# Unit outputs by token halves through three PSUM banks, convolution taps in the fourth, earlier U loads

## The chip, the cores and the metric

One core of a Trainium2 chip runs the whole kernel. The metric is the device time of one launch in microseconds (us), the median over several runs.

## The reference, cut to what matters

One inference step of a two-layer decoder trunk on a prompt of 512 tokens and 8 sample tokens. Each layer normalises the residual, projects it by one wide matrix `w_in`, feeds three branches (a state-space branch A, a convolution branch B, cross-attention X) and merges them by gates:

```
h = rmsnorm(x, norm_g)
u_a, z_a, u_b, z_b, q, z_x, g_a, g_b, g_x = split(h @ w_in)
y_a, s_new = s5_branch(u_a, ...)                 # 32 groups, 64 complex states, scan over positions
y_a = gelu(y_a); y_a = y_a * sigmoid(y_a @ w_glu + b_glu)
o_a = (y_a * silu(z_a)) @ w_br_ssm
v_b = u_b[:, :512] * sigmoid(u_b[:, 512:])
c_b = silu(layernorm(causal_depthwise_conv(v_b, width 31)))
o_b = (c_b * silu(z_b)) @ w_br_conv
prob = softmax(q @ mk.T * scale); o_x = (prob @ mv * silu(z_x)) @ w_br_xatt
m = sigmoid(g_a) * o_a + sigmoid(g_b) * o_b + sigmoid(g_x) * o_x
x = x + m @ w_out
```

The layer is done for the prompt and for the samples with the same weights; `mk`, `mv` are projections of a 256-token memory for the prompt and caches for the samples. A last rmsnorm gives the outputs; the new states, convolution buffers and memory keys and values are outputs too.

## The kernel before, in words

**Layout.** Activations are transposed: channels on 128 partitions, tokens along the free axis, in two token halves of 260 (256 of the prompt and 4 samples). `h` and every weight are split into a high and a low part in fp32r, and a product is the sum high by high, low by high, high by low.

**Units.** The product of `h` with 128 columns of `w_in` is a unit: 8 k tiles x 3 parts x 2 token halves = 48 matmuls of 260 columns. `PAIRS` (L283) lists the units of a layer in pairs, named by their kind: v (convolution input and its gate), q, u (state-space input), e (gates of the branches B and X), x, b, a (the `z` paths). After them come the tail (the gates of A and the branch products, in four rounds) and the output product. `split_product` (L716) issues a unit; at each k tile and part it does both token halves with the same weight. Its result goes to `acc_ps[0]` or `acc_ps[1]` in turn, each two PSUM banks, one for each token half; `acc_ready0/1` and `acc_free0/1` are the semaphores. `mp`, the other four banks, serves everything that is not a unit.

**The weight ring.** SyncE loads half a unit of weights into one of four slots of `w_st` (`ring_load`, L350), ScalarE casts it to `w_hi` (`high`, L1145), GpSimd makes `w_lo` (`low`, L605, the subtraction at L610). A load waits until `w_lo` of the slot's earlier content is made, a cast until TensorE has used the slot (`w_half_used` for the first half of a unit, `acc_ready` for the second).

**Orders written by hand.** Each engine works through its own list in order, and what a layer's work stands between is decided there. TensorE's list runs through the units and puts the other work between them: memory keys and values, scores and their transposes, the sample attention (`spread`, `sample_products`, `turn_sample`), the state-space work in two halves of the groups (`turn_inputs`, `state_inputs`, `lag_matrices`, `outputs`). ScalarE (`ready` L1150, `one`, `pair`) casts the ring's next half, waits for a unit, casts another half and evacuates both token halves in one instruction (`to_gate`, `to_q`, `to_u`, `to_z`, `to_v`, `glu_gate`). VectorE's list holds the softmax, the state-space matrices and scans, the convolution and the merge.

**The convolution** (`convolution`, L1641) makes 31 taps per channel tile of 512 prompt tokens: at k = 0 `tensor_scalar`, else `scalar_tensor_tensor` through the helper at L1457. Even taps add into one half of `cacc`, odd ones into the other, both in SBUF, so that two neighbours don't depend on each other (`behind=1`); a last addition puts both sums together into `cv`. The taps are cut into pieces between VectorE's other work (`taps_between`), and some pieces wait at `low_made` until a given `w_lo` is there.

**SyncE's list** holds all other loads too, at the places where the code has them. The state-space input `u` goes through DRAM: `u_scratch` is stored after the u units, and twelve loads with a small row each put it into `U` (L464 to L467), behind the value caches of the samples (`cache_load`); they wait until GpSimd has cleared the borders of `U`. The lag matrices go through `k_scratch` into `Mt` (`toeplitz`, L469 to L481), the state-space output through `y_scratch` back into `u` (L505 to L509), and b1's second unit is loaded behind that.

Of the kernel before, what the change touches and what calls it, by code (L numbers as in the profile page):

```python
# [21 lines left out]
P = 128  # L22
# [3 lines left out]
NB = 8  # L26
# [46 lines left out]
def build(nc, x_prompt, x_sample, mem_prompt, state_ssm_re, state_ssm_im, state_conv, cache_mem_k,  # L73
# [12 lines left out]
    with ctx:  # L86
# [54 lines left out]
        def rr(name, off, shape):  # L141
# [60 lines left out]
        t1 = rr("t1", 10256, [P, QH * (T + 1) * H])  # L202
        t2 = rr("t2", 11408, [P, QH * (T + 1) * H])
# [14 lines left out]
        cacc = at(wd_at, 16 * P, 24 * P, "cacc", [P, 2, T, C])  # L218
# [52 lines left out]
            br_x_done=1 glu_sg=4 br_a_done=4 gate_sg=8 sg_free=16 m_done=8 x_sum=8 z_ev=1 b_ready=24 b_free=24 acc_ready0=32  # L271
            acc_ready1=32 acc_free0=32 acc_free1=32 d_loaded0=80 d_loaded1=80
# [3 lines left out]
        acc_ready, acc_free, d_loaded = ([sm[f"{n}{i}"] for i in range(2)] for n in ("acc_ready", "acc_free", "d_loaded"))  # L276
# [15 lines left out]
        assert unit["out"] + KT == UNITS and use["out"] + KT // 2 == per["acc_ready0"]  # L292
# [24 lines left out]
        def _(sp):  # L317
# [42 lines left out]
            for l in range(LAYERS):  # L360
# [75 lines left out]
                pair("e1")  # L436
                half("e2", 0)
                for b in range(4, NB - 2):
                    wait(sp, l, "kq_done", b - 3)
                    cache_load(cache_mem_k, b)  # L440
                half("e2", 1)
                for b in range(NB - 2, NB):
                    wait(sp, l, "kq_done", b - 3)
                    cache_load(cache_mem_k, b)
# [8 lines left out]
                half("x1", 0)  # L453
# [5 lines left out]
                wait(sp, l, "u_out", 16)  # L459
                wait(sp, l, "U_clear", 1)  # L460
                ug = u_dram.rearrange("(g h) a c -> h g a c", h=H)
                Ug = U[:, :, :, :].rearrange("p q e c -> p (q e) c")
                for t in range(T):
                    sp.dma_start(Ug[t * H:(t + 1) * H, :, NB:NB + C], ug[:, :, t // 4, (t % 4) * C:(t % 4 + 1) * C]).then_inc(sm["U_in"], 16)  # L464
                for a in range(2):
                    sp.dma_start(Ug[0:H, :, 4 * a:4 * a + 4], ug[:, :, a, 4 * C:HC]).then_inc(sm["U_in"], 16)
                    sp.dma_start(Ug[7 * H:P, :, YC + 4 * a:YC + 4 * a + 4], ug[:, :, a, 4 * C:HC]).then_inc(sm["U_in"], 16)  # L467

                def toeplitz(half):  # L469
# [3 lines left out]
                    kg = kh.rearrange("g h x -> h g x")  # L473
                    sp.dma_start(kh.rearrange("(r y) h x -> (y h) r x", r=2), kt[:, :, :]).then_inc(sm["k_out"], 16)
# [12 lines left out]
                pair("e5")  # L487
                pair("e6")
                pair("e7")
                pair("b0")  # L490
                pair("a0")
# [8 lines left out]
                pair("a1")  # L500
# [11 lines left out]
                def glu_loads():  # L512

                    wait(sp, l, "acc_done", 4)
# [81 lines left out]
        def _(pool):  # L596
# [7 lines left out]
            for l in range(LAYERS):  # L604
# [35 lines left out]
                for name in ("u1", "e0", "e1", "e2", "x0"):  # L640
# [3 lines left out]
                wait(pool, l, "pv_done", 1)  # L644
                wait(pool, l, "V_done", 1)
                pool.memset(U[:, :, :, 0:NB], 0.0)
# [1369 lines left out]
```

## Time and profile before

| | |
|---|---|
| median of 3 runs | 1162.32 us (1159.71 to 1163.3) |
| the profiled execution's own time | 1161.13 us |
| its span in the profile | 1159.3 us |
| TensorE matmuls / VectorE / ScalarE / GpSimd busy | 94% / 72% / 36% / 37% of the span |
| granted TensorE clock, mean | 0.975 |

A busy share counts the time in which an instruction of the engine was under way. TensorE's matmuls are pipelined: one takes 0.29 us from its start to its modelled end, while the next starts 0.12 us after it. A wait is put down to the engine and line whose semaphore came last; "DVEq" is VectorE's sequencer (an increment without an instruction), "SPq" the DMA issues of SyncE, "issue" a time in which the profile shows no other releaser. Line numbers can be those of a helper: L1451 is every `tensor_tensor`, L1457 every `scalar_tensor_tensor`, L659 every transpose, L729 every unit product.

### The profile page before, as it was taken

To read this page: it belongs to the slowest core of one execution; us is meant where nothing else is said; L and a number is where in the kernel's file an instruction comes from. 1 tells how busy PE (TensorE), PEld (TensorE's weight loads), DVE (VectorE), ACT (ScalarE), POOL (GpSimd) and SP (SyncE) were. 2 spreads that over 40 slices of the span, in tenths; PEclk is the share of its full clock that TensorE was granted. 3 is DMA by queue.
4 is the path that set the end of the run, shared out by engine and by line. 5 is a ranking of instruction groups with operands and counts; after the bars stand their busy time and mean duration, and the time that the engine had idled before them with its cause. 6 is when DMAs were issued, how large, how long until landed. Compare 5 with 4: busy or idle time off the path is not lost.

```text
span 1159.3 us, 20485 instructions
## 1 busy us (share of the span) xinstructions
PE 1084.3 (94%) x8274; PEld 1015.6 (88%) x8274; DVE 834.0 (72%) x1209; ACT 415.8 (36%) x709; POOL 427.9 (37%) x329
## 2 busy tenths in 40 slices
PE   5999899989989899999989999998998999899995
PEld 3679889979979889999956999897997989899994
DVE  3899989868996684444677998987899668644412
ACT  5423443325443252222433354332535334222222
POOL 0245443524332223444403644353332331344440
PEclk9999999989999999999999999999998999899998
DMA  9345427594317813445532651669531573344422
GB/s 259 100 100 189 145 74 213 191 167 121 99 42 148 231 62 115 130 129 155 152 98 82 173 181 50 196 205 168 133 110 56 124 182 119 103 123 136 135 83 74
DMA packets 225269, 155.01 MB, mean 134 GB/s; under 512 B 48651, under 2 KB 201675, under 8 KB 223111
## 3 DMA queue, kind: packets, MB, share of 16 engines
q1 hardware_dynamic: 219590, 142.04, 44.4%
q10 hardware_dynamic: 5584, 11.67, 2.8%
q8 instruction: 65, 1.06, 0.4%
q14 instruction: 30, 0.24, 0.1%
HBM read 130.38 MB, written 24.24 MB: 133 GB/s over the span
## 4 chain that ended last, share of the span: by engine, by line
PE 51%; DVE 31%; SPq 6%; DMA 6%; issue 4%; ACT 2%; POOL 0%; DVEq 0%; ACTq 0%
PE acc L729 29%; PE mp L1071 12%; DVE cacc L1457 10%; DVE s L1451 4%; DVE X L1451 3%; DMA w_st<-in_w_in 3%; PE mp L768 2%; SPq L464 2%; PE mp L659 2%; DVE tiny L1451 2%; PE acc L1052 1%; SPq L505 1%; PE mp L874 1%; DVE wt L1451 1%; DMA y_scratch<-U 1%
## 5 line engine op out<-in xcount | busy, mean ns | idle before, releaser
L610 POOL TENSOR_TENSOR w_lo<-w_st,w_hi 128x512 fp32r<-128x512 f32 x288 | 403.3, 1406 | 654.4 <-ACT w_hi L1148 654.0
L1148 ACT CAST w_hi<-w_st 128x512 fp32r<-128x512 f32 x288 | 177.6, 622 | 574.1 <-PE acc L729 352.8
L729 PE MATMUL acc<-h_hi,w_hi 128*128 128x260 f32 x1600 | 332.0, 289 | 6.8 <-ACT z L1293 5.9
L729 PE MATMUL acc<-h_hi,w_lo 128*128 128x260 f32 x1600 | 325.2, 285 | 0.0
L729 PE MATMUL acc<-h_lo,w_hi 128*128 128x260 f32 x1600 | 325.1, 285 | 0.0
L729 PEld LDWEIGHTS acc<-h_hi,w_hi 128*128 128x128 f32 x1600 | 250.8, 191 | 15.8 <-issue 7.7
L729 PEld LDWEIGHTS acc<-h_lo,w_hi 128*128 128x128 f32 x1600 | 249.9, 191 | 0.0
L729 PEld LDWEIGHTS acc<-h_hi,w_lo 128*128 128x128 f32 x1600 | 249.9, 191 | 0.0
L1457 DVE SCALAR_TENSOR_TENSOR cacc<-vx,cw,cacc 128x512 f32<-128x512 f32 x232 | 222.7, 1021 | 10.3 <-POOL w_lo L610 7.0
L1071 PE MATMUL mp<-br_hi,w_hi 128*128 128x260 f32 x384 | 79.1, 288 | 6.2 <-DVEq L1933 3.9
L1071 PE MATMUL mp<-br_lo,w_hi 128*128 128x260 f32 x384 | 78.7, 287 | 0.0
L1071 PE MATMUL mp<-br_hi,w_lo 128*128 128x260 f32 x384 | 78.6, 287 | 0.0
L1071 PEld LDWEIGHTS mp<-br_hi,w_hi 128*128 128x128 f32 x384 | 60.7, 193 | 6.6 <-issue 6.6
L1451 DVE TENSOR_TENSOR mj<-mp,xT 128x520 f32<-128x520 f32 x16 | 11.2, 700 | 76.8 <-PE mp L1071 75.9
L768 PE MATMUL mp<-wkv,memg 128*128 128x512 f32 x128 | 60.3, 620 | 4.0 <-DMA wkv<-in_w_k 2.8
L1071 PEld LDWEIGHTS mp<-br_hi,w_lo 128*128 128x128 f32 x384 | 60.8, 193 | 0.0
L1071 PEld LDWEIGHTS mp<-br_lo,w_hi 128*128 128x128 f32 x384 | 60.6, 193 | 0.0
L768 PEld LDWEIGHTS mp<-wkv,memg 128*128 128x128 f32 x128 | 24.5, 199 | 34.5 <-issue 25.7
L1451 DVE TENSOR_TENSOR xT<-acc,xT 128x520 f32<-128x520 f32 x16 | 11.2, 700 | 56.2 <-PE acc L729 56.2
L729 PE MATMUL acc<-m_lo,w_hi 128*128 128x260 f32 x256 | 51.6, 283 | 0.0
L729 PE MATMUL acc<-m_hi,w_hi 128*128 128x260 f32 x256 | 51.6, 283 | 0.0
L729 PE MATMUL acc<-m_hi,w_lo 128*128 128x260 f32 x256 | 51.5, 283 | 0.0
(300 smaller groups left out, 1408.2 us busy)
## 6 DMA issues: line engine op xcount, KB each, us to landing
w_st<-in_w_in SPq DMA_DIRECT2D x208, 256.0 KB, 3.2
g_scratch<-xT ACTq DMA_DIRECT2D x32, 260.0 KB, 3.2
xT<-g_scratch SPq DMA_DIRECT2D x8, 1040.0 KB, 6.6
kb<-in_cache_mem_k SPq DMA_DIRECT2D x16, 512.0 KB, 4.2
kb<-in_cache_mem_v SPq DMA_DIRECT2D x16, 512.0 KB, 5.1
w_st<-in_w_out SPq DMA_DIRECT2D x32, 256.0 KB, 2.8
x_scratch<-xT SPq DMA_DIRECT2D x2, 2080.0 KB, 7.6
xT<-x_scratch SPq DMA_DIRECT2D x4, 1040.0 KB, 5.9
```

The costliest lines, as they stand in the source:

```text
L464: sp.dma_start(Ug[t * H:(t + 1) * H, :, NB:NB + C], ug[:, :, t // 4, (t % 4) * C:(t % 4 + 1) * C]).then_inc(sm["U_in"], 16)
L505: sp.dma_start(yg[:, :, t // 4, (t % 4) * C:(t % 4 + 1) * C], Ug[t * H:(t + 1) * H, :, NB:YC]).then_inc(sm["y_out"], 16)
L610: pool.tensor_tensor(w_lo[:, slot, :], w_st[:, slot, :], w_hi[:, slot, :].bitcast(F32), ALU.subtract).then_inc(w_staged_free, 1)
L659: return pe.transpose(out, in_, ident[0:n, 0:n])
L729: last = pe.matmul(acc_ps[pair][:, a, 0:HC], w[:, slot, kk * P:(kk + 1) * P], x[:, k, a, :], start=(k == 0 and p == 0), stop=(k == KT - 1 ...
L768: last = pe.matmul(mp[:, 2 * (1 - i // 4) + m, :], memg[:, k, m * P:(m + 1) * P], wkv[:, i % 2, kk * E:(kk + 1) * E], start=(k == 0), stop ...
L874: last = pe.matmul(mp[:, hd, :], vtok[:, m, hd * P:(hd + 1) * P], pT[:, hd, m, :], start=(m == 0), stop=(m == 1))
L1052: last = pe.matmul(acc_ps[j][:, a, 0:HC], w_dir[:, g, k * 2 * P + j * P:k * 2 * P + (j + 1) * P], u[:, k, a, :], start=(k == 0), stop=(k = ...
L1071: last = pe.matmul(mp[:, 2 * jj + a, 0:HC], w[:, slot, c0:c0 + P], y[:, x, k, a, :], start=(k == 0 and i == 0), stop=(k == ET - 1 and i == 2))
L1148: act.copy(w_hi[:, c % SLOTS, :], w_st[:, c % SLOTS, :]).then_inc(w_hi_done, 1)
L1451: run(dve.tensor_tensor(out, a, b, op), behind)
L1457: run(dve.scalar_tensor_tensor(out=out, in0=a, scalar=s, in1=b, op0=op0, op1=op1), behind)
```

## The change

- A unit's two token halves are made one after the other, 24 matmuls each, and every half is handed on alone. The halves take three PSUM banks in turn (`bank`); `acc_ready` and `acc_free` are one semaphore each, counted by halves (`ordinal`, `credits`). The first half of a weight slot is released after the second token half has used it. The first output unit alone keeps the old order of the halves (`together`).
- ScalarE evacuates half by half, and casts the next half of the ring behind each (`half`). In the output product VectorE adds half by half.
- The fourth bank holds the sum of the taps (`taps_sum`): each tap adds to it and waits for the one before, and a copy takes it out. The stops on `w_lo` are gone and the pieces of the convolution are cut at other taps. `cacc` is gone, so the gate weights of the GLU wait for the lag matrices' store and no longer for the convolution. In the tail the fourth bank takes halves, too.
- SyncE: the U loads go behind e1, between the units and the key and value caches; U is cleared behind e0 and the attention product, the temporaries `t1`, `t2` make room for it. The lag matrices' stores go ahead of the weights of e4 and of a1's first unit, their reading back stays behind it.
- TensorE transposes the memory before the parameters, and two products of memory keys stand before the second layer's square sums.

```diff
@@ the banks
+        def ordinal(use_n, k, a=0):
+            return 4 * use_n + 2 * k + a
+        def bank(l, i):
+            late = i - ordinal(use["glu"], 0)
+            if i == 3 or late >= 0 and late % 4 == 0:
+                b = 3
+            else:
+                b = (l * per["acc_ready"] + (i if late < 0 else i - late // 4 * 4 - 4)) % 3
+            return acc_ps[b // 2][:, b % 2, 0:HC]
+        def credits(i):
+            return i + 1 if i < ordinal(use["glu"], 0) else i
...
+        taps_sum = acc_ps[1][:, 1, :].rearrange("p (t c) -> p t c", c=C)
@@ SyncE
+                pair("e1")
+                wait(sp, l, "u_out", 16)
+                wait(sp, l, "U_clear", 1)
+                prompt_rows(0, 3)
                 half("e2", 0)
+                prompt_rows(3, 5)
+                keys(4)
                 half("e2", 1)
+                keys(5)
+                prompt_rows(5, 7)
                 half("x0", 0)
+                keys(6)
+                keys(7)
+                prompt_rows(7, 8)
+                sample_rows(0)
+                half("x0", 1)
                 for b in range(2):
                     wait(sp, l, "kq_done", b + 5)
                     cache_load(cache_mem_v, b)
-                half("x0", 1)
+                half("x1", 0)
                 for b in range(2, 4):
                     wait(sp, l, "kq_done", b + 5)
                     cache_load(cache_mem_v, b)
-                half("x1", 0)
+                sample_rows(1)
                 half("x1", 1)
                 half("e3", 0)
...
                 half("e3", 1)
+                lags_out(0)
                 half("e4", 0)
                 toeplitz(0)
                 half("e4", 1)
...
+                lags_out(1)
+                half("a1", 0)
                 toeplitz(1)
...
-                    wait(sp, l, "acc_done", 4)
+                    wait(sp, l, "k_out", 32)
@@ GpSimd
+                wait(pool, l, "pv_done", 1)
+                pool.memset(U[:, :, :, 0:NB], 0.0)
+                pool.memset(U[:, :, :, YC:UC], 0.0).then_inc(sm["U_clear"], 1)
+                for name in ("e1", "e2", "x0"):
+                    pair(name)
@@ TensorE
+                    for h, kk, a in ((h, kk, a) for a in range(2) for h in range(2) for kk in range(HK)):
...
+                        if k == 0 and not together:
+                            wait(pe, l, "acc_free", credits(i + a))
...
+                                last = pe.matmul(bank(l, i + b), w[:, slot, kk * P:(kk + 1) * P], x[:, k, b, :],
+                                                 start=(k == 0 and p == 0), stop=(k == KT - 1 and p == 2))
+                                if k == KT - 1 and p == 2:
+                                    last.then_inc(acc_ready, 1)
+                        if kk == HK - 1 and h == 0 and (a or together):
+                            last.then_inc(w_half_used, 1)
@@ ScalarE
+                def half(name, k, a, evac):
+                    n = l * UNITS + unit[name] + k
+                    wait(act, l, "acc_ready", ordinal(use[name], k, a) + 1)
+                    evac(int(name[1]), k, a)
+                    if a == 0:
+                        act.wait_ge(w_half_used, halves(l, unit[name] + k) + 1)
+                    high(2 * n + a + SLOTS)
@@ VectorE
-                        o = cacc[:, k % 2, :, :]
                         if k == 0:
-                            ts(o, src, w, vec[:, 20 + i:21 + i], ALU.mult, ALU.add, behind=1)
-                        elif k == 1:
-                            run(dve.tensor_scalar(o, src, w, None, ALU.mult), behind=1)
+                            ts(taps_sum, src, w, vec[:, 20 + i:21 + i], ALU.mult, ALU.add)
                         else:
-                            stt(o, src, w, o, ALU.mult, ALU.add, behind=int(k < end - 1))
+                            stt(taps_sum, src, w, taps_sum, ALU.mult, ALU.add)
...
+                        run(dve.tensor_copy(cv[:, i, 0, :, 0:4 * C], acc_ps[1][:, 1, :].rearrange("p (a c) -> p a c", a=2)))
...
-                taps_between(0, 0, [(tap, "q0", n // 2, n % 2) for n, tap in enumerate((16, 20, 24, 28) if l == 0 else (8, 13, 18, 23))], TAPS)
-                taps_between(1, 0, [(4, "q1", 1, 0), (8, "q1", 1, 1), (12, "v2", 0, 0)], 14)
+                convolution(0, 0, TAPS)
+                convolution(1, 0, 18)
                 scores_max(0)
...
-                convolution(1, 14, 19)
+                convolution(1, 18, 24)
                 scores_max(1)
                 probabilities(0)
...
-                convolution(1, 27, TAPS)
-                taps_between(2, 0, [(6, "e0", 0, 0)], 12)
+                convolution(2, 0, 20)
...
-                taps_between(3, 12, [(12, "e7", 1, 1), (16, "b0", 0, 0), (21, "b0", 0, 1), (26, "b0", 1, 0)], TAPS)
+                convolution(3, 22, TAPS)
                 take_inputs(1)
```

## Rows read from the trace of the kernel before

**Rows 1.** The page's engines: busy us, share of the span, instructions.

```profile
PE 1084.3 (94%) x8274; PEld 1015.6 (88%) x8274; DVE 834.0 (72%) x1209; ACT 415.8 (36%) x709; POOL 427.9 (37%) x329
```

**Rows 2.** Waits of TensorE: total us, times, longest us.

```profile
PE mp L958 <- issue: 11.1, 2, 5.6
...
PE mp L659 <- ACT oxs L1341: 9.8, 2, 5.5
PE mp L659 <- DVEq L1637: 6.2, 3, 4.4
PE acc L729 <- ACT z L1293: 5.9, 2, 3.1
...
PE mp L1071 <- DVEq L1933: 3.9, 1, 3.9
PE mp L776 <- DVEq L1968: 3.4, 1, 3.4
...
PE mp L1071 <- POOL w_lo L610: 2.3, 1, 2.3
```

**Rows 3.** Stretches: length, busy us of each engine (instructions), clock, DMA, GB/s.

```profile
460.00:480.00 20.00, 20.00 (x169) 20.00 (x168) 10.78 (x12) 4.87 (x8) 9.09 (x7) 1.00 0.31 93
...
125.90:130.40 4.50, 0.21 (x2) 0.00 (x1) 4.23 (x7) 1.51 (x7) 0.00 (x0) 1.00 0.49 211
131.40:137.10 5.70, 5.70 (x37) 5.70 (x36) 5.49 (x6) 3.97 (x5) 3.72 (x3) 0.70 0.32 94
...
253.70:259.50 5.80, 5.80 (x36) 5.80 (x34) 3.41 (x8) 1.24 (x2) 1.41 (x2) 0.66 1.21 194
```

**Rows 4.** Groups by form: busy us, mean ns; idle us before, releaser.

```profile
L610 POOL TENSOR_TENSOR w_lo<-w_st,w_hi 128x512 fp32r<-128x512 f32 x288 | 403.3, 1406 | 654.4 <-ACT w_hi L1148 654.0 <-POOL v_s L624 0.4
...
L1457 DVE SCALAR_TENSOR_TENSOR cacc<-vx,cw,cacc 128x512 f32<-128x512 f32 x232 | 222.7, 1021 | 10.3 <-POOL w_lo L610 7.0
...
L1451 DVE TENSOR_TENSOR mj<-mj,tj 128x520 f32<-128x520 f32 x32 | 45.2, 1414 | 6.2 <-DVE tj L1451 3.9
...
L1940 DVE TENSOR_TENSOR m_lo<-mj,m_hi 128x520 fp32r<-128x520 f32 x16 | 11.2, 701 | 0.6
...
L1451 DVE TENSOR_TENSOR mj<-mp,xT 128x520 f32<-128x520 f32 x16 | 11.2, 700 | 76.8 <-PE mp L1071 75.9 <-DVE br_lo L1743 0.4 <-DVE mj L1451 0.4
```

**Rows 5.** VectorE in the first layer: instructions on `cacc` in a stretch; timeline.

```profile
72.40:106.10 33.70, 33.39 (x32) 1.00 0.54 153
...
121.51 1.23 DVE L1628 TENSOR_REDUCE stat<-mp 128x4 f32<-128x1024 f32 x1
...
129.15 1.23 DVE L1451 TENSOR_TENSOR pr<-pr,stat 128x1024 f32<-128x1024 f32 x1
...
315.82 17.94 DVE L1457 SCALAR_TENSOR_TENSOR cacc<-vx,cw,cacc 128x512 f32<-128x512 f32 x19
...
334.52 1.92 DVE L1795 COPY X<-mp 64x288 f32<-64x288 f32 x4
```

**Rows 6.** SyncE's timeline, first layer: start, us, issue, count.

```profile
229.13 11.64 SPq L464 DMA_DIRECT2D U<-u_scratch  x8
...
245.07 3.33 SPq L353 DMA_DIRECT2D w_st<-in_w_in  x4
...
347.44 0.37 SPq L474 DMA_DIRECT2D k_scratch<-kt  x1
...
368.24 6.88 SPq L505 DMA_DIRECT2D y_scratch<-U  x8
...
382.58 2.86 SPq L353 DMA_DIRECT2D w_st<-in_w_in  x4
```

**Rows 7.** The chain that ended last, in order of time: start, us, work.

```profile
4.52 5.83 DMA drow<-in_ssm_d
...
12.10 3.51 PE acc L659 x16
```

More of the change, by code:

```diff
@@ L291, in build, with evacuated @@
         use["out"] = use["ga"] + 4
-        assert unit["out"] + KT == UNITS and use["out"] + KT // 2 == per["acc_ready0"]
+        assert unit["out"] + KT == UNITS and 4 * use["out"] + 2 * KT == per["acc_ready"]
+        def ordinal(use_n, k, a=0):
[9 more added lines that the diff above has]
+            return i + 1 if i < ordinal(use["glu"], 0) else i
+        def evacuated(eng, l, use_n, k):
+            wait(eng, l, "acc_free", ordinal(use_n, k, 1) + 4)
         def halves(l, n):
@@ L486, in _ @@
                 half("e4", 1)
[L487 to L491, printed above, removed]
+                for name in ("e5", "e6", "e7", "b0", "a0"):
+                    pair(name)
+                lags_out(1)
+                half("a1", 0)
                 toeplitz(1)
@@ L743, in first_pair @@
                     n = l * UNITS
-                    for k in range(2):
-                        wait(pe, l, f"acc_free{k}", use["v0"] + 1)
+                    wait(pe, l, "acc_free", 3)
                     for k in range(KT):
@@ L1075, in _ @@
                 for j in range(KT):
-                    split_product(j % 2, use["out"] + j // 2, l * UNITS + unit["out"] + j, m_hi, m_lo, "m_done")
+                    split_product(j % 2, use["out"] + j // 2, l * UNITS + unit["out"] + j, m_hi, m_lo, j == 0)
                     if j == 3 and l + 1 < LAYERS:
@@ L1156, in ready @@
                         high(c + SLOTS)
-                    wait(act, l, f"acc_ready{k}", use_n + 1)
+                    wait(act, l, "acc_ready", ordinal(use_n, k, 1) + 1)
                     if more:
                         high(c + SLOTS + 1)
+                def half(name, k, a, evac):
[5 more added lines that the diff above has]
+                    high(2 * n + a + SLOTS)
                 def one(name, k, evac):
-                    ready(k, use[name], unit[name] + k)
-                    evac(int(name[1]), k)
+                    for a in range(2):
+                        half(name, k, a, evac)
                 def pair(name, evac):
@@ L1291, in to_z, with evac @@
                 def to_z(x):
-                    def evac(it, k):
-                        act.activation(tile(z[:, x, :, :, :], it * 2 + k), acc_ps[k][:, :, 0:HC], ACT.Silu).then_inc(acc_free[k], 1)
+                    def evac(it, k, a):
+                        name = f"{'abx'[x]}{it}"
+                        act.activation(z[:, x, it * 2 + k, a, :], bank(l, ordinal(use[name], k, a)), ACT.Silu).then_inc(acc_free, 1)
                     return evac
+                half("x0", 0, 0, to_z(2))
                 wait(act, l, "nbs_done", 1)
@@ L1298, in _ @@
                                accum_out=stat[0:32, 49:50]).then_inc(sm["exps_done"], 1)
-                one("x0", 0, to_z(2))
+                half("x0", 0, 1, to_z(2))
+                wait(act, l, "acc_ready", ordinal(use["x0"], 1, 0) + 1)
+                to_z(2)(0, 1, 0)
                 ready(1, use["x0"], unit["x0"] + 1)
@@ L1945, in _ @@
                 for j in range(KT):
-                    wait(dve, l, f"acc_ready{j % 2}", use["out"] + j // 2 + 1)
                     wait(dve, l, f"slots_in{j // 4}", 48)
-                    xj = xT[:, j, :, :]
-                    tt(xj, acc_ps[j % 2][:, :, 0:HC], xj, ALU.add)
-                    dve.sem_inc(acc_free[j % 2], 1)
+                    for a in range(2):
+                        o = ordinal(use["out"], j, a)
+                        wait(dve, l, "acc_ready", o + 1)
+                        tt(xT[:, j, a, :], bank(l, o), xT[:, j, a, :], ALU.add)
+                        dve.sem_inc(acc_free, 1)
                     dve.sem_inc(sm["x_sum"], 1)
```

192 lines of the change are left out of this document (92 added, 100 removed).

## The prediction

> **What bounds the kernel now.** I read the page's engine shares first: TensorE is busy for 1084.3 of 1159.3 us [rows 1], so time can only come out of the gaps of its stream. The waits of TensorE name them [rows 2]. Seven lines, 42.6 us in all: the lag matrices of the second half (11.1, both layers), the transposes that wait for the sample attention's product `oxs` (9.8), the ones that wait for normalised probabilities (6.2 over three places), a unit product behind an evacuation of `z` (5.9), the square sums between the layers (3.4), and the branch products (3.9 and 2.3). The table by stretch shows what a gap costs afterwards [rows 3]. At the granted clock of 1.00, its level of 2.4 GHz, 20 us hold 169 matmuls, 0.118 us each, so 5.7 to 5.8 us hold 48 or 49. After 4.4 us in which the engine did nothing, the next 5.7 us were granted 0.70 on average (part of them at the 1.2 GHz level) and held 37. After the `oxs` wait 5.8 us were granted 0.66 and held 36. A gap of this size thus costs some 1.4 us more, twelve matmuls at 0.118.
>
> Why the gaps are there, from the other engines. **VectorE** makes the convolution's taps, and its timeline in the first layer [rows 5] shows the taps of the first channel tile in 72.4 to 106.1, fourteen of the next, and only then the maxima of the first scores (121.5) and the probabilities (129.15 to 130.4), while TensorE has run dry at 126.1 (125.9 plus 0.21 busy, [rows 3]). Later 19 taps fill 315.8 to 333.8, the state inputs are copied out behind them until 336.4, and the lag matrices wait for that. The taps are slow because of a collision [rows 4]: a tap reads two operands of SBUF and takes 1.02 us on average. In the tail, too, two SBUF operands (`mj<-mj,tj`) take 1.41 us, but the same shape with one operand in PSUM (`mj<-mp,xT`) takes 0.70 us, with GpSimd at its `w_lo` subtractions in both cases. **SyncE's queue** explains `oxs` [rows 6]: twelve U loads, the eight of the row and four for the samples, hold it from 229.13 to 245.07, and the weights of unit e3 issue behind them. ScalarE stands at its cast of those weights before it can copy `oxs`.
>
> **The change, part by part.**
>
> *Taps into PSUM.* Removed: two SBUF accumulators, alternating, and the sum of the two. Added: one chain of 31 dependent instructions in the fourth bank and one copy out. No row shows VectorE writing PSUM. From below: 0.69 us, the 520-wide `mj<-mp,xT` scaled to 512 columns; nothing gains on it, since `m_lo` from two SBUF operands with little collision takes the same 0.701. From above: a read pass and a write pass one after the other, 1.40. I take 0.69, the row with one operand in PSUM, plus 0.04 for the wait on the predecessor (idle of 0.6 us over sixteen `m_lo`, which wait for theirs): 0.73. A channel tile then takes 31 x 0.73 + 0.7 = 23.3 us instead of 33.7.
>
> *Probabilities.* Before the first probabilities VectorE now needs 31 + 24 = 55 taps. Beside them stand two maxima at 1.4, the probabilities at 1.4, and I estimate 3.4 for the small copies at a tile's start, the copy out and the query remainder: 7.6. From 72.4: 72.4 + 55 x 0.73 + 7.6 = 120.2, against the 126.1 at which TensorE wants them. The 5.9 to spare go partly into waits for the scores themselves. The gap closes for any tap up to (126.1 - 72.4 - 7.6) / 55 = 0.84 us. Second layer alike: **6.2**, and 1.4 of clock in the first.
>
> *Lag matrices.* In front of the second state inputs stand 9 taps instead of 19: 9 x 0.73 = 6.6 against 17.9, 11 us off a wait of 5.5 to 5.6 per layer. What is late next is TensorE's own order. **11.1**, and twice 1.4.
>
> *U loads.* They move behind attention, in groups of three, two, two and one, with the sample rows after. The queue waits there for U's clearing, which GpSimd now does after e0's low halves and the attention product; behind that in GpSimd's queue stand only e1's subtractions, due a unit later. Each U load takes about (245.07 - 229.13) / 12 = 1.3 us of the queue, so a group delays the key and weight loads behind it by up to 4 us; those weights are held back by their ring anyway, and the keys by VectorE's reading of the earlier ones. The weights of e3 then issue about 16 us earlier: **9.8** goes, and twice 1.4. The lag stores go ahead of their reading back, so k_scratch's round trip (issue 347.44) no longer holds the a1 weights.
>
> *The `z` wait.* Unit b1's weights stand behind the ten y stores and their landing (368.24 to 382.58). That order stays, but the GELU in front is freed earlier by the a1 weights. I take 3 of the 5.9, and 1 of clock: **4**.
>
> *Between the layers, start and end.* One more key product in front of the square sums covers their 3.4 us; the normalisation behind them then paces the next product. I take **2.5**. At the start, the memory transposes stood until 12.10 behind the parameters, whose last load landed at 10.35 [rows 7]; without it I estimate **2**. The last unit leaves half of a 0.70 us addition behind its end: **0.3**.
>
> *Halves.* Each unit ends as two halves of 24 matmuls, 2.9 us. With three banks a half waits for the evacuation of the half three before it; the two halves between take 5.8 us, as the other unit did with two double banks. The rows show that taking banks in turn costs nothing at that depth: 460 to 480, all unit and branch products, holds 169 matmuls at a clock of 1.00 [rows 3]. The Trainium skill, "TensorE: Matmul & The Clock Gate", section on psum-queue depth-cycling, speaks against it: a kernel that takes PSUM banks in turn let TensorE idle for moments between groups, often enough that its clock kept falling and rising. By the row the halves add nothing to the sum; by that rule they make rival (d). The first half of a weight slot is released at three quarters of the unit instead of at its middle, 1.4 us later; a subtraction of 1.41 us and a cast must follow within the seven that are left. I cost both at nothing. If the cover went, each late half would cost its lateness. ScalarE evacuates twice per unit and is otherwise mostly idle. The moved temporaries and the earlier gate weights cost nothing: the lag wait that replaces theirs ends long before.
>
> **Sum:** 6.2 + 11.1 + 9.8 = 27.1 of waits, 5 x 1.4 = 7 of clock, then 4 + 2.5 + 2 + 0.3: 42.9. I take 2 back for ties in the scans, whose results now arrive just as TensorE asks. The profiled execution took 1161.1 us (span 1159.3); 1161.1 - 40.9 = 1120.2, and the median of the runs lies 1.2 above it: **1121 us**. The branch products' 6.2 stay, because the layer norm's chain on VectorE is unchanged.
>
> **Rivals.** (a) *The U loads collide where they go:* they delay keys and values, and the e3 weights are late again. The 9.8 and their 2.8 of clock stay: 1134. For it speaks that each load spends 1.3 us in the queue; against it the slack of 16 us. 0.14. (b) *The taps still collide*, so the change doesn't do what it says: a `w_lo` every 2.9 us costs some 0.7 us (1.41 against 0.70), a quarter of VectorE's time; 55 taps and the 7.6 then take 63 us instead of 48, and the probabilities come at 135.4, 5 us later than now in each layer. The lag gap still closes, for ten taps fewer stand before it. 40.9 - 6.2 - 1.4 - 10 leaves 23: 1139. Sixteen undisturbed `mj<-mp,xT` speak against it. 0.07. (c) *Slower: the in-place tap in PSUM reads and writes in two passes.* Its place is the probabilities. Against now, the gap grows by 55 x (tap - 0.92) in each layer, 0.92 being what gives today's 130.4. It decides when 110 x (tap - 0.92) is over the 33 gained elsewhere, from 1.22 us per tap. At 1.44 it is 57 - 33 = 24 slower: 1186. No row has such an output, but none with PSUM is slow. 0.09. (d) *Slower: the halves starve.* ScalarE evacuates late at every unit, the clock falls, and each of the 120 unit products loses the 1.4 us of [rows 3]: 168 us, 1289. The depth of 5.8 us speaks against it, and it decides only when evacuations come later than that. 0.02.
>
> **Numbers.** About 0.3%, 3.5 us, is what a measurement can tell from no change. Forecast 0.62, (a) 0.14, (b) 0.07, (c) 0.09, (d) 0.02, and 0.06 for something unseen, most of it around no change. Faster 0.85, same 0.04, slower 0.11. The low end, 1106, takes in that the branch waits and all of the `z` wait go too (6.2 + 2.9 and their clock). The high end, 1146, takes in (a), (b) and some late halves on top.
>
> **What would show it.** Taps of 0.7 to 0.75 us each, all alike, and `w_lo` near 1.3. No waits of TensorE on the probabilities, on `oxs` or before the lag matrices; those on the branch products still there. U loads before the value loads. Wrong would be taps over 0.9, new waits of the unit products for evacuations, or a clock below 1.00 in the middle of a layer.

## The result and the profile after

The changed kernel took 1119.43 us (median of four runs, 1118.15 to 1123.03) against 1161.86 for the kernel before: a ratio of 0.9641, 95% interval 0.9613 to 0.9669. The forecast was 1121. A second measurement of it, in a later group of runs, gave a ratio of 0.9659 (0.9635 to 0.9682). The profiled execution took 1118.15 us, its span 1116.3.

The page's engines and its two groups of interest, to be held against [rows 1] and [rows 4] (L1532 are the taps, L651 GpSimd's subtractions):

```profile
PE 1075.5 (96%) x8274; PEld 1006.7 (90%) x8274; DVE 794.8 (71%) x1225; ACT 437.0 (39%) x823; POOL 412.2 (37%) x329
...
L651 POOL TENSOR_TENSOR w_lo<-w_st,w_hi 128x512 fp32r<-128x512 f32 x288 | 393.0, 1369 | 623.3 <-ACT w_hi L1202 619.9
...
L1532 DVE SCALAR_TENSOR_TENSOR acc<-vx,cw,acc 128x512 f32<-128x512 f32 x240 | 181.4, 756 | 9.8
```

TensorE's idle time fell from 75.0 us (1159.3 - 1084.3) to 40.8, and its busy time by 8.8, for the same matmuls at a mean granted clock of 0.986 instead of 0.975. Its waits after the change, total, times and longest, against [rows 2]:

```profile
PE mp L1125 <- POOL w_lo L651: 5.0, 2, 2.5
...
PE mp L821 <- DMA wkv<-in_w_k: 3.8, 2, 3.5
PE mp L1030 <- DVEq L1886: 3.4, 2, 1.7
...
PE mp L702 <- DVE ps L1834: 1.9, 2, 1.0
...
PE mp L829 <- DVEq L2024: 0.7, 1, 0.7
```

The waits on the probabilities, on `oxs`, before the lag matrices and on `z` are gone, and the square sums' is 0.7 instead of 3.4. The branch products (L1125) still wait. Behind the start two lines are new: the second output matrices wait for the scan's `x_done` (L1030), and the transposes of the sample probabilities wait for their normalisation (L702).

VectorE in the first layer, against [rows 5] (timeline: start, us, instruction, count):

```profile
72.28 0.81 DVE L1529 TENSOR_SCALAR acc<-vx,cw,vec 128x512 f32<-128x512 f32 x1
73.13 23.71 DVE L1532 SCALAR_TENSOR_TENSOR acc<-vx,cw,acc 128x512 f32<-128x512 f32 x30
96.88 0.69 DVE L1733 COPY cv<-acc 128x512 f32<-128x512 f32 x1
...
112.90 1.22 DVE L1702 TENSOR_REDUCE stat<-mp 128x4 f32<-128x1024 f32 x1
...
123.24 0.18 DVE L1709 RECIPROCAL stat<-stat 128x4 f32<-128x4 f32 x1 [1.27 <-ACT pr L1315]
123.45 1.22 DVE L1526 TENSOR_TENSOR pr<-pr,stat 128x1024 f32<-128x1024 f32 x1
```

A channel tile takes 25.3 us (72.28 to 97.57) where it took 33.7, and VectorE itself now waits 1.27 us for the exponentials in front of the first probabilities.

SyncE in the first layer, against [rows 6] (timeline): the U loads come in groups from 169.41, among the other loads, and the first two weight loads of e3 (the last two of the four in the last row) are issued by 220.2 instead of from 245.07:

```profile
169.41 1.40 SPq L465 DMA_DIRECT2D U<-u_scratch  x3
175.06 2.62 SPq L376 DMA_DIRECT2D w_st<-in_w_in  x2
177.72 1.04 SPq L465 DMA_DIRECT2D U<-u_scratch  x2
...
207.76 12.38 SPq L376 DMA_DIRECT2D w_st<-in_w_in  x4
```

**Where the time went.** Both kernels issue 8274 matmuls, in nearly the same order, so the start of the n-th can be compared between the two traces. The lengths below are differences of such starts. They hold the wait, the clock after it, and nothing that lies elsewhere.

| place (matmuls n to n) | layer 1, before to after | layer 2, before to after | sum | forecast |
|---|---|---|---|---|
| probabilities (600-900; 4650-4950) | 44.1 to 38.1 | 41.1 to 38.9 | -8.2 | -7.6 |
| sample probabilities (1350-1500; 5400-5550) | 15.2 to 16.1 | 15.2 to 16.3 | +2.1 | part of +2 |
| `oxs` (1500-1800; 5550-5850) | 43.8 to 35.6 | 41.8 to 35.6 | -14.4 | -12.6 |
| lag matrices (2250-2400; 6300-6450) | 22.3 to 15.3 | 22.9 to 15.3 | -14.6 | -13.9 |
| second outputs (2400-2550; 6450-6600) | 17.5 to 24.1 | 18.5 to 22.8 | +11.0 | part of +2 |
| `z`, unit b1 (2550-2700; 6600-6900) | 24.6 to 19.6 | 50.4 to 45.7 | -9.6 | -4 |
| branches (2700-3000; 6900-7200) | 48.2 to 46.9 | 42.4 to 38.8 | -5.0 | 0 |
| between the layers (4050-4350) | 63.3 to 60.4 | | -2.9 | -2.5 |
| start (0-600) | | | -0.1 | -2 |
| everything else | | | -1.3 | -0.3 |

The sum is -43.0. In a second profile of the changed kernel (e9) these lengths agree within 0.3 us, but for the sample probabilities (15.4 in each layer, so +0.4 in all) and the first layer's branches (48.2, as before the change). Two large numbers of opposite sign stand in it that the forecast had not: +11.0 at the second outputs, -9.6 at `z`. Stretches behind a gap show what the clock adds (length, TensorE's busy us and matmuls, clock, DMA, GB/s), to be read with [rows 3]:

```profile
414.37:417.15 2.78, 0.28 (x4) 1.00 0.33 94
417.15:422.95 5.80, 5.80 (x48) 1.00 0.17 48
...
291.60:295.16 3.56, 3.56 (x32) 1.00 0.27 72
341.96:348.77 6.81, 6.81 (x32) 0.50 0.11 30
...
341.96:351.70 9.74, 9.74 (x45) 0.50 0.10 24
```

Behind the new gap of 2.00 us (339.96 to 341.96) the 32 output products of 72 columns take 6.81 us at 1.2 GHz; the same 32 of the first half of the groups took 3.56 (291.60 to 295.16). The 1.2 GHz lasts from 341.4 to 351.6. The 45 matmuls in the 9.74 us behind the gap would take 5.1 at full clock (32 at 0.111 and 13 at 0.12), so the clock costs 4.6 us, more than the gap. Behind the branches' gap of 2.78 us the clock stayed at 1.00 in this execution.

### The profile page after: what moved, and what is told of

It reads as the page before. It is cut to its first block, busy times and chain, and to the rows that moved or that the text cites. A ratio compares the mean times of both kernels' runs of the same rounds, so it can differ in the third digit from the quotient of the medians.

```text
span 1116.3 us, 20527 instructions
## 1 busy us (share of the span) xinstructions
PE 1075.5 (96%) x8274; PEld 1006.7 (90%) x8274; DVE 794.8 (71%) x1225; ACT 437.0 (39%) x823; POOL 412.2 (37%) x329
## 4 chain that ended last, share of the span: by engine, by line
PE 79%; DVE 14%; DMA 3%; issue 1%; ACT 1%; POOL 1%; SPq 0%; DVEq 0%; ACTq 0%
PE acc L778 50%; PE mp L1125 12%; PE mp L821 3%; PE acc L1106 3%; PE mp L702 2%; DVE X L1526 2%; DVE s L1526 2%; PE mp L1030 2%; DMA kb<-in_cache_mem_k 1%; PE mp L998 1%; PE mp L889 1%; PE mp L927 1%; DVE ht L1532 1%; DVE V L1526 1%; DVE tiny L1526 1%
## 5 line engine op out<-in xcount | busy, mean ns | idle before, releaser
L651 POOL TENSOR_TENSOR w_lo<-w_st,w_hi 128x512 fp32r<-128x512 f32 x288 | 393.0, 1369 | 623.3 <-ACT w_hi L1202 619.9
L778 PE MATMUL acc<-h_hi,w_hi 128*128 128x260 f32 x1600 | 459.3, 287 | 0.0
L778 PE MATMUL acc<-h_hi,w_lo 128*128 128x260 f32 x1600 | 453.1, 283 | 0.0
L778 PE MATMUL acc<-h_lo,w_hi 128*128 128x260 f32 x1600 | 452.8, 283 | 0.0
L778 PEld LDWEIGHTS acc<-h_hi,w_hi 128*128 128x128 f32 x1600 | 302.5, 189 | 7.7 <-issue 5.0
L778 PEld LDWEIGHTS acc<-h_hi,w_lo 128*128 128x128 f32 x1600 | 302.5, 189 | 0.7 <-issue 0.5
L778 PEld LDWEIGHTS acc<-h_lo,w_hi 128*128 128x128 f32 x1600 | 302.6, 189 | 0.0
L1532 DVE SCALAR_TENSOR_TENSOR acc<-vx,cw,acc 128x512 f32<-128x512 f32 x240 | 181.4, 756 | 9.8
L1125 PE MATMUL mp<-br_hi,w_hi 128*128 128x260 f32 x384 | 77.4, 283 | 5.0 <-POOL w_lo L651 5.0
L1125 PE MATMUL mp<-br_lo,w_hi 128*128 128x260 f32 x384 | 77.4, 283 | 0.0
L1125 PE MATMUL mp<-br_hi,w_lo 128*128 128x260 f32 x384 | 77.2, 283 | 0.0
L778 PE MATMUL acc<-m_hi,w_hi 128*128 128x260 f32 x256 | 69.7, 282 | 0.0
L778 PE MATMUL acc<-m_hi,w_lo 128*128 128x260 f32 x256 | 69.6, 282 | 0.0
L1125 PEld LDWEIGHTS mp<-br_hi,w_hi 128*128 128x128 f32 x384 | 59.1, 188 | 5.4 <-issue 5.4
L1125 PEld LDWEIGHTS mp<-br_hi,w_lo 128*128 128x128 f32 x384 | 59.3, 188 | 0.0
L1125 PEld LDWEIGHTS mp<-br_lo,w_hi 128*128 128x128 f32 x384 | 59.2, 188 | 0.0
L821 PEld LDWEIGHTS mp<-wkv,memg 128*128 128x128 f32 x128 | 24.6, 199 | 38.0 <-issue 29.0
L1526 DVE TENSOR_TENSOR X<-X,s 128x16 f32<-128x16 f32 (+9 forms) x88 | 51.3, 583 | 3.0
```

The lines of the kernel that those rows point to most:

```text
L651: pool.tensor_tensor(w_lo[:, slot, :], w_st[:, slot, :], w_hi[:, slot, :].bitcast(F32), ALU.subtract).then_inc(w_staged_free, 1)
L778: last = pe.matmul(bank(l, i + b), w[:, slot, kk * P:(kk + 1) * P], x[:, k, b, :], start=(k == 0 and p == 0), stop=(k == KT - 1 and p == 2))
L821: last = pe.matmul(mp[:, 2 * (1 - i // 4) + m, :], memg[:, k, m * P:(m + 1) * P], wkv[:, i % 2, kk * E:(kk + 1) * E], start=(k == 0), stop ...
L1125: last = pe.matmul(mp[:, 2 * jj + a, 0:HC], w[:, slot, c0:c0 + P], y[:, x, k, a, :], start=(k == 0 and i == 0), stop=(k == ET - 1 and i == 2))
L1526: run(dve.tensor_tensor(out, a, b, op), behind)
L1532: run(dve.scalar_tensor_tensor(out=out, in0=a, scalar=s, in1=b, op0=op0, op1=op1), behind)
```

## The experiments

Each kernel is the changed kernel with the edit shown. Ratios are to the kernel before on the same chip, with 95% intervals; 0.01 is 11.6 us.

| run | median us | ratio | interval |
|---|---|---|---|
| e1_taps_in_sbuf | 1146.33 | 0.9909 | 0.9877 to 0.9942 |
| e2_pairs_taps_in_sbuf | 1150.89 | 0.9947 | 0.9919 to 0.9975 |
| e3_u_loads_late | 1131.31 | 0.9771 | 0.9750 to 0.9791 |
| e4_outputs_mid_unit | 1118.48 | 0.9660 | 0.9645 to 0.9674 |
| e5_old_tap_counts | 1137.20 | 0.9780 | 0.9741 to 0.9818 |
| e6_y_path_short | 1113.24 | 0.9581 | 0.9551 to 0.9611 |
| e7_lag_stores_old_place | 1115.43 | 0.9598 | 0.9563 to 0.9634 |
| e8_turns_and_keys_old_order | 1126.05 | 0.9699 | 0.9663 to 0.9734 |
| e9_changed_again | 1122.17 | 0.9659 | 0.9635 to 0.9682 |
| e10_a1_behind_lags | 1113.92 | 0.9596 | 0.9575 to 0.9616 |
| e11_scan_b1_probs | 1111.78 | 0.9573 | 0.9552 to 0.9593 |
| e12_all_four | 1132.43 | 0.9748 | 0.9727 to 0.9769 |

**e1: taps back in SBUF.**

```diff
-stt(taps_sum, src, w, taps_sum, ALU.mult, ALU.add)
+o = cacc[:, k % 2, :, :]
...
+stt(o, src, w, o, ALU.mult, ALU.add, behind=int(k < end - 1))
...
+wait(sp, l, "acc_done", 4)
```

> The changed kernel in everything but the home of the taps: they go back into two SBUF accumulators taken in turn, with the sum of the two at the end. The output weights' loads then also wait until the accumulators are free. Theory (the home of the taps carries the probabilities' part): a tap takes 1.0 to 1.05 us on average again instead of 0.756, so the 55 taps in front of the first probabilities take about 14 us more; they were ready some 2 us before TensorE asked, so a wait of 9 to 12 us returns in each layer, with the clock after it: 1138 to 1148 us. The taps ahead of the second state inputs (9) cost only 2 us more, and VectorE stood 2.7 us there, so nothing new before the lag matrices. Rival (the order and the U loads carry the gain, the taps' home little): within 4 us of the changed kernel, 1116 to 1123.

The home of the taps alone, in this kernel without stops on `w_lo`, is worth 0.025 to 0.027 of the time, some 30 us. By position the largest losses are 10.1 us at the first layer's probabilities (matmuls 600 to 900) and 9.7 in the second layer, but there at a unit ahead of them (4350 to 4650); the second layer's probabilities lose nothing. (The profiled execution of e1 took 1153.56 us, 7 over the median.) Waits of TensorE in e1:

```profile
PE acc L780 <- POOL w_lo L653: 9.5, 3, 7.9
PE mp L704 <- DVEq L1713: 7.7, 1, 7.7
```

GpSimd's and VectorE's timeline in a stretch of the second layer of e1:

```profile
627.82 14.36 POOL L653 TENSOR_TENSOR w_lo<-w_st,w_hi 128x512 fp32r<-128x512 f32 x1 [14.45 <-ACT w_hi L1204]
...
627.73 13.33 DVE L1534 SCALAR_TENSOR_TENSOR cacc<-vx,cw,cacc 128x512 f32<-128x512 f32 x20
```

In the first layer VectorE is late with the probabilities, as forecast. In the second, VectorE runs at full pace and GpSimd starves: one subtraction, 1.3 us elsewhere, takes 14.36 us, until the taps are over, and TensorE waits 7.9 us for the weights. The kernel before held taps back until a subtraction was done, which this kernel does not. The Trainium skill, "SBUF — State Buffer", section "Who interferes with whom", states that a VectorE instruction with two SBUF inputs and a GpSimd instruction that reads SBUF shut each other out, the second to issue blocking until the first finishes. The trace agrees that they exclude each other; but here the wait spans 20 taps, not one.

The spread of the taps' durations (a tile's instructions: ns, least/median/most), first in the kernel before:

```profile
L1457 DVE SCALAR_TENSOR_TENSOR cacc<-vx,cw,cacc x232: 737/748/1830, 73.3 to 887.1; 128x512 f32<-128x512 f32 x116
```

In the changed kernel:

```profile
L1532 DVE SCALAR_TENSOR_TENSOR acc<-vx,cw,acc x240: 737/756/757, 73.1 to 845.6; 128x512 f32<-128x512 f32 x120
```

In e1:

```profile
L1534 DVE SCALAR_TENSOR_TENSOR cacc<-vx,cw,cacc x232: 732/744/1844, 75.0 to 875.9; 128x512 f32<-128x512 f32 x116
```

A tap in SBUF that nothing disturbs takes 744 to 748 ns, and with two accumulators the next starts 0.67 us later (20 in 13.33 us). A tap in PSUM is no faster: 756 ns, and 0.79 us from start to start. What PSUM buys is that none of 240 is disturbed and that GpSimd goes on.

**e2: units in pairs of banks again, taps in SBUF.** Against e1:

```diff
-if i == 3 or late >= 0 and late % 4 == 0:
...
-    b = (l * per["acc_ready"] + (i if late < 0 else i - late // 4 * 4 - 4)) % 3
+b = i % 4
...
+together = True
```

> As the first of these kernels (taps in SBUF), and the unit outputs back in pairs of banks, four banks in turn by twos, both token halves of a unit multiplied with each weight. Against the first it differs in the halves alone. Theory (taking three banks in turn by halves costs nothing): within 4 us of the first kernel, and no new waits of TensorE on evacuations in either. Rival (the halves starve TensorE or drop its clock a little at each unit): this kernel is faster than the first by 10 us or more, and its busy time of TensorE is smaller.

The intervals of e1 and e2 overlap. In five units that follow one another, matmuls 1757 to 1997, where the halves take three banks in turn, the kernel with pairs takes 28.9 us and those with halves (e1 and the changed kernel) 28.7. In the tail, matmuls 3000 to 3900, where halves take the fourth bank too, it is 108.1 and 107.9. Taking the banks in turn by halves costs nothing there.

**e3: U loads behind the value loads**, with their waits.

```diff
-prompt_rows(0, 3)
...
-sample_rows(1)
...
 cache_load(cache_mem_v, b)
+wait(sp, l, "u_out", 16)
+wait(sp, l, "U_clear", 1)
+prompt_rows(0, 8)
+sample_rows(0)
+sample_rows(1)
```

> The changed kernel with the twelve U loads back behind the last value load, in one block. Theory (they held the weights of e3 and so the copy of oxs): TensorE waits again some 5 us per layer for oxs, 9 to 10 in all, with 2 to 5 of clock; the key loads come earlier, so the wait on the normalised sample probabilities (1.9 in the changed kernel) goes: 1127 to 1133 us. Rival (the loads only changed their victim, keys for weights): within 4 us of the changed kernel.

As the theory has it: 1131.31. The wait on the sample probabilities is gone, and in the waits of TensorE in e3 the one on `oxs` is back:

```profile
PE mp L699 <- ACT oxs L1409: 8.6, 2, 4.5
```

By position `oxs` costs 7.8 and 5.8 us, clock included. VectorE's idle time before its key products is 3.6 us here and 9.7 in the changed kernel, 6.6 of that for key loads: rival (a) names a real collision, but its price is at most the 1.9 us of the sample probabilities (the second profile of the changed kernel, e9, has no such wait), not the 9.8 of `oxs`.

**e4: the second outputs in the middle of a1.**

```diff
-outputs(1)
-one("a1", 0)
+one("a1", 0, lambda: outputs(1))
```

The function is called between the token halves.

> The changed kernel with the second output matrices (outputs of half 1) moved from in front of unit a1's first product into its middle, behind its first token half, 2.9 us of TensorE's work later. Theory (TensorE waits 1.7 us twice for x_done there, in gaps of 2.0 and 1.9 us, and the clock lies at the 1.2 GHz level for 10.2 and 6.8 us behind them, in which 45 matmuls ran where 86 fit at 1.00): both gaps close and the clock stays: 3 to 4 of waits and 4.8 + 3.4 of clock, 1106 to 1111 us. Rival (what comes behind is late instead: the y copies, the stores of y, the layer norm, all 2.9 us later): 1116 to 1123 us, with a new wait of TensorE further on.

By position 6.8 and 5.4 us are gained at the outputs, as the theory has it, and the total does not move. What came, in the waits of TensorE in e4:

```profile
PE acc L780 <- POOL w_lo L651: 3.6, 2, 1.9
...
PE mp L702 <- DVE ps L1835: 2.8, 2, 2.0
```

The first is unit b1, in gaps of 2.2 and 2.1 us: its weights stand on SyncE behind the y stores and their landing, and TensorE now reaches them earlier. So part of the `z` term of the table is no gain in itself: by position 4.8 of its 9.6 us are lost again here, because TensorE no longer waits at the outputs. The other 4.8 stay. (The start, unedited, was 3.3 us longer in this execution.)

**e5: the old cut of the taps.**

```diff
-convolution(1, 0, 18)
+convolution(1, 0, 14)
...
-convolution(3, 22, TAPS)
+convolution(3, 12, TAPS)
```

> The changed kernel with the taps still in PSUM, but cut as before: 50 taps instead of 55 in front of the first probabilities, and 19 instead of 9 in front of the second state inputs. Theory (with fast taps the cut decides only where a chain of VectorE ends last): no wait on the probabilities, since fewer taps stand there; ten taps of 0.792 us from start to start put the second state inputs 7.9 us later, of which 2.7 are idle now, so 5.2 us more per layer reach TensorE, partly before the lag matrices and the rest on x_done: 10 to 11 us in all, 1127 to 1132. Rival (the speed alone made the gain, the cut is immaterial): within 4 us of the changed kernel.

1137.20, more than the theory's 1132. Its first step is right (the lag matrices wait 1.7 us in each layer, the probabilities not at all), but the late second half shows as waits on the lag matrices' reading back (`Mt<-k_scratch`, 4.5 in two), with the clock at 1.2 GHz for 13.7 and 17.1 us behind, and the sample probabilities cost 3.3 and 5.1 by position (the old cut has three taps in front of the sample maximum and not behind it). The order of the taps is worth some 15 us with fast taps.

**e7 and e10: which part shortens or lengthens the scan.** e7 puts the lag stores and a1's weights back; e10 moves a1's weights alone.

```diff
 lags_out(1)
-half("a1", 0)
 toeplitz(1)
 ...
-half("a1", 1)
+pair("a1")
```

> The changed kernel with the lag stores and their reading back together again, behind e4's first half and ahead of both halves of a1. Theory (a1's weights behind the store's round trip delay ScalarE's cast in front of the second GELU, and with it the y stores and b1's weights): a wait on b1's product of 2 to 3 us returns in each layer, with some clock: 1123 to 1130 us. Rival (the wait on b1's product went because everything before it on VectorE is earlier now): within 4 us of the changed kernel.

> The changed kernel with one edit: the first half of a1's weights issues behind the reading back of the second lag stores instead of ahead of it; the first lag stores stay ahead. Theory (a1's weights, early, put two more low-half subtractions of GpSimd beside the second scan, whose 59 instructions then take 27.6 us of VectorE instead of 25.7, so x_done comes 2 us after TensorE asks and the clock falls behind the gap): the scan takes 25.7 again, no wait on x_done in either layer, 1114 to 1117 us. Rival (the early reading back of the first lag stores is what costs): as the changed kernel.

e7's theory falls: with the old order the kernel is faster, not slower. Unit products wait 2.9 us for low halves in three places, but the wait on `x_done` is gone. e10 shows why, 8.3 us faster than the changed kernel on the same chip. VectorE in the second scan of each layer, by stretches (length, busy us and instructions, clock, DMA, GB/s), in the changed kernel, where the window holds one 0.27 us instruction more:

```profile
312.30:342.10 29.80, 27.58 (x59) 0.99 0.52 114
849.70:879.50 29.80, 27.57 (x59) 1.00 0.52 114
```

The same in e10:

```profile
312.80:340.50 27.70, 25.48 (x58) 1.00 0.42 83
846.70:874.40 27.70, 25.47 (x58) 1.00 0.41 84
```

Where the time goes, in the first layer of the changed kernel, VectorE and GpSimd:

```profile
331.69 1.71 DVE L1526 TENSOR_TENSOR X<-X,s 128x112 f32<-128x112 f32 x2
333.43 1.58 DVE L1526 TENSOR_TENSOR s<-X,lv 128x240 f32<-128x240 f32 x1
...
331.87 1.28 POOL L651 TENSOR_TENSOR w_lo<-w_st,w_hi 128x512 fp32r<-128x512 f32 x1 [4.62 <-ACT w_hi L1202]
333.35 1.29 POOL L651 TENSOR_TENSOR w_lo<-w_st,w_hi 128x512 fp32r<-128x512 f32 x1 [0.20 <-ACT w_hi L1202]
```

VectorE in e10, where GpSimd has no subtraction between 327.8 and 342.4:

```profile
332.21 0.79 DVE L1525 TENSOR_TENSOR X<-X,s 128x112 f32<-128x112 f32 x2
333.03 0.59 DVE L1525 TENSOR_TENSOR s<-X,lv 128x240 f32<-128x240 f32 x1
```

The early weights bring two more subtractions beside the scan, whose additions and products have both operands in SBUF, and the same work takes 1.8 us longer. Of the 58 instructions that both kernels have there, only two differ by more than 0.1 us, in each layer: the two that run beside those subtractions (1.3 instead of 0.4, and 1.6 instead of 0.6). So this part of the change is a loss: without it 6.5 and 5.1 us go at the outputs by position, gap and clock, of which 1.2 and 1.6 come back at b1.

**e8: transposes and key products in the old order.**

```diff
+param_turns(0)
+wait(pe, 0, "par_ev", 1)
 def memory_turns(j):
...
-key_values(0, 2)
+key_values(0, 1)
 square_sums()
-key_values(2, 4)
+key_values(1, 4)
```

> The changed kernel with the parameter transposes in front of the memory's again, and one key product instead of two in front of the square sums between the layers. Theory (by TensorE's position the start gained nothing, since the key products wait for their weights further on, and the passage between the layers gained 2.9 us): the start stays, the square sums wait 3 us again, 1120 to 1124 us. Rival (the forecast's 2 us at the start are there): another 2 us, 1122 to 1126.

The start is the same within 0.2 us at matmul 300. Between the layers TensorE waits 4.2 us for the square sums, where it waited 0.7, and the passage is 4.1 longer by position. The rest of the profiled difference, nearly 5 us, comes for the most part in three pieces of 1.4 to 1.7 at unedited places, where the clock fell behind gaps that are in both kernels. The total, 1126, lies in the rival's range, for another reason than the rival's.

**e6, e9, e11, e12: versions put together.** e6 is e4 with b1's weights ahead of the y stores and three taps behind the sample probabilities; e11 is the last two edits with the lag stores and a1's weights of e7; e12 is e11 with the outputs of e4; e9 is the changed kernel unedited.

```diff
 half("b1", 0)
+half("b1", 1)
 wait(sp, l, "y_ev", 8)
...
-convolution(2, 20, 23)
...
-convolution(2, 23, TAPS)
+convolution(2, 20, TAPS)
```

> The kernel with the second output matrices in the middle of unit a1's first product, with two more edits: the second half of b1's weights is loaded in front of the y stores instead of behind their landing, and the three taps between the sample maximum and the normalised sample probabilities go behind those. Theory (the gain of that kernel, 6.8 and 5.4 us at the outputs by TensorE's position, was given back by b1's weights, 2.2 us twice with 1.8 and 0.4 of clock, and by the sample probabilities): the outputs' 12.2 us stay gained and 1 to 2.5 us more on the sample probabilities, so 1103 to 1108 us where the changed kernel takes 1119. Rival (the chain of the y stores and the layer norm behind them sets the end of this stretch whatever is in front): 1112 to 1119, with a new wait on y_in, the layer norm or the branch inputs.

> The changed kernel itself, unedited, for a comparison on the same chip. 1116 to 1122 us.

> The changed kernel with the lag stores back at their old place, the second half of b1's weights in front of the y stores, and the three taps behind the normalised sample probabilities; the second output matrices stay in front of a1. Theory (each edit takes away a wait that a trace of this study shows: x_done 2.0 and 1.9 with their clock, b1's low halves 1.4 and 1.6, the sample probabilities 2.6 and 2.1 where the lag stores alone were moved): 1108 to 1111 us. Rival (the transposes of the sample probabilities and the layer norm take the place of what goes): 1113 to 1117.

> As the kernel before, and the second output matrices in the middle of unit a1's first product as well. Theory (with the scan shortened x_done comes when TensorE asks, so nothing is left to gain there, while the y stores and the layer norm start 2.9 us later): 1 to 4 us slower than that kernel, with a longer wait on the branch inputs. Rival (the margin helps still): 1 to 3 us faster.

e6 took 1113.24, short of its theory: the outputs' gain stayed (6.8 and 5.4 by position) and b1's wait was gone, but 2.9 us came back in the second layer's branches, 3.0 at the first layer's sample products and 2.7 at the start. e9 was measured on the chip of e10, e11 and e12. e11, 1111.78, has the lowest median: 10.4 us under the changed kernel beside it, 0.9573 of the kernel before, so it beats both; its interval overlaps those of e6, e7 and e10. It misses its theory by 1 us; what came in its place is a branch wait. From the waits of TensorE in e11:

```profile
PE mp L1124 <- DVEq L1986: 3.9, 1, 3.9
PE mp L1124 <- POOL w_lo L650: 2.5, 1, 2.5
...
PE mp L968 <- ACT psT L1373: 0.9, 1, 0.9
```

e12 contradicts both theories, 20.7 us slower than e11. The first of TensorE's waits in e12:

```profile
PE acc L779 <- POOL w_lo L650: 14.6, 2, 7.7
```

With a1's weights late (e11) the outputs in front of a1 cover them; with the outputs inside a1 (e4) nothing does, and TensorE waits 7.2 and 8.0 us at a1. Each edit is sound alone; together they take each other's cover.

## Why the prediction was right, and where it was not

The total was forecast at 1121 and came at 1119.43. Of its steps:

- **Taps.** The price, 0.69 plus 0.04, is too low: 0.756 plus 0.036 of gap. The step that failed is the choice of the row: `mj<-mp,xT`, another operation. The undisturbed tap stood in the kernel before, 748 ns as the median of a form whose mean of 1021 mixed two populations; the forecast read the mean. It did little harm, as 0.792 is under the 0.84 that closes the gap, but the first probabilities stood at 124.7 and not at 120.2, 1.2 us ahead of their transposes. That all taps are alike and `w_lo` is near 1.3 is as forecast; "the taps are slow because of a collision" left out that GpSimd is starved in turn, 9.7 us of the second layer's loss in e1. Rivals (b) and (c) fall with 240 undisturbed taps.
- **Probabilities**, -7.6 forecast, -8.2 measured. e1 confirms the cause in the first layer (-6.0); in the second (-2.2) the probabilities are in time in e1 too, and what the taps in SBUF delay there is GpSimd.
- **Lag matrices**, -13.9 and -14.6. The cut at nine taps closes the wait alone, as in e1 with its taps in SBUF (15.3 in each layer); fast taps alone, with 19 in front (e5), gain 11 of the 14.6. The step "what is late next is TensorE's own order" failed: VectorE's scan, whose end the wait on the lag matrices had covered, was next, 2 us late, and its gap cost +11.0 with the clock. I took 2 us "for ties in the scans"; the place was right and the size a fifth. What made the scan late is another part of the change, a1's early weights, whose effect on the scan the forecast put at nothing: with them late (e10) the outputs take 17.6 and 17.7, about as in the kernel before.
- **U loads**, -12.6 and -14.4, confirmed by e3. The collision with the keys is there too (+2.1, but +0.4 in e9). An issue spread among other work costs less than the 1.3 us I took: 0.49 us as the median of the sixteen row loads.
- **The lag stores and `z`.** The mechanism I gave for -4, that a1's weights free the GELU earlier, fell with e7 and e10: those weights lengthen the scan, and with them late 6.9 of the 9.6 are still there. The rest is the other side of the +11.0 at the outputs: where those waits were removed (e4, e7, e10), b1 waited 1.2 to 2.2 us again and 4.8, 2.7 and 2.7 of the 9.6 came back. What gained the part that stays no run tells.
- **Between the layers**, -2.5 and -2.9; e8, where the wait returns, prices it at 4.1. **Start**, -2 and -0.1: e8 shows that the first unit comes at the same time with either order, since the key products behind still wait for their weights.
- **Branches**, forecast 0, measured -5.0: the second layer's wait is shorter (3.9 before, on banks that VectorE frees behind the layer norm's chain; 2.5 after, on `w_lo`), and the clock does not fall behind it; the first layer's 1.3 is clock alone and missing in e9. In e6 and e11, which wait neither at the outputs nor at b1, the 3.9 on VectorE is back. That those waits had covered it fits, but no run separates it.
- **Halves**, nothing forecast and nothing found (e2). Rival (d), by the rule of the Trainium skill, "TensorE: Matmul & The Clock Gate", section on psum-queue depth-cycling, does not hold here: with three banks taken in turn for 240 matmuls the stretch takes 28.7 us, with pairs 28.9.

The forecast's comparison in the tail was misread: GpSimd was not at its subtractions "in both cases". Durations in the kernel before (ns, least/median/most):

```profile
L1451 DVE TENSOR_TENSOR mj<-mj,tj x32: 700/1628/1707, 440.8 to 1095.9; 128x520 f32<-128x520 f32 x32
L1451 DVE TENSOR_TENSOR mj<-mp,xT x16: 699/700/700, 434.5 to 1082.3; 128x520 f32<-128x520 f32 x16
```

Eight of the 32 `mj<-mj,tj`, those beside no subtraction, took 0.70 us too, and only one of the sixteen `mj<-mp,xT` (434.54) ran beside one throughout. So these rows said little for the operand in PSUM; the 240 taps show it.

So the three main terms were right in mechanism and within 2 us in size. That the rest came out right is luck: errors of +11 (outputs and sample probabilities) and +2 (start) met errors of -5.6 (`z`) and -5 (branches).

## What to carry to other kernels

Price an instruction from the spread of its own durations: a mean over a form can hide an undisturbed population and a disturbed one, and moving one operand out of SBUF may buy peace for the other engine rather than speed. When several waits on one stream are removed, look for the chain that each of them covered, and count what the clock loses behind the gap that is left, here 4.6 us behind a gap of 2.0. Loading weights earlier is not free if another engine then works on them beside a critical chain.

## What was not expected of the hardware

- One GpSimd subtraction of 1.3 us took 14.36 us beside a stream of VectorE instructions with two SBUF operands (e1).
- The size of a gap does not settle what the clock does. After 2.00 us, with 72-column matmuls ahead of it, TensorE ran at 1.2 GHz for 10.2 us; after the branches' 2.78 us, behind 260-column matmuls, it kept 1.00 in the first profile of the changed kernel, and in the second, of the same kernel, the same gap was followed by fewer matmuls (stretches of TensorE in e9, the gap and then what follows):

```profile
413.46:416.24 2.78, 0.29 (x3) 0.94 0.33 94
416.24:422.04 5.80, 5.80 (x37) 0.73 0.18 48
```

- A product with its result in PSUM (the first tap, 814 ns) is slower than into SBUF (548 ns as the median in the kernel before); a tap, which also reads the accumulator, differs by 8 ns.
